# Gate steps of the expert stage on TensorE: run in pairs behind two U blocks each, instead of one behind each U block

## The reference, cut to what matters

```
def block(xb):
    qh = (xb @ w_pq).reshape(PEER_BLOCK, PEER_HEADS, 2, PEER_HALF)
    s = jnp.einsum('thcd,ckd->thck', qh, sub_keys).astype(jnp.float32)
    s_top, i_top = lax.top_k(s, PEER_TOPK)
    cand = (s_top[:, :, 0, :, None] + s_top[:, :, 1, None, :]).reshape(...)
    best, ci = lax.top_k(cand, PEER_TOPK)
    e = (i_top of half 0 at ci // 16) * N_KEYS + (i_top of half 1 at ci % 16)
    gw = jax.nn.softmax(best, axis=-1)
    act = jax.nn.gelu(jnp.einsum('tkd,td->tk', u_tab[e], xb)) * gw
    return jnp.einsum('tk,tkd->td', act, v_tab[e])
```

## Time and profile before

| | us |
|---|---|
| median of 2 runs | 2036.71 |
| the two runs | 2034.24 and 2039.18 |
| the profiled execution | 2032.12 |
| its span, first to last instruction | 2030.4 |

### The profile page before, as it was taken

One profiled execution on the slowest core, in us unless ns is written; L12 is line 12 of the kernel. 1 busy time (PEld: TensorE's weight loads), 2 busy tenths in 40 slices (PEclk: granted clock), 3 DMA queues, 4 the chain that ended last, 5 costly groups with the idle time before them and its releaser, 6 DMA issues.

```text
span 2030.4 us, 28703 instructions
## 1 busy us (share of the span) xinstructions
PE 1912.2 (94%) x10526; PEld 1606.1 (79%) x10526; DVE 1356.0 (67%) x2554; ACT 726.4 (36%) x967; POOL 706.6 (35%) x506
## 2 busy tenths in 40 slices
PE   5999977597999999999999999999999999999998
PEld 4999544386888888888888878878888888888886
DVE  4343658465198887779679787457666666666676
ACT  3113117441234453453455345423232232232232
POOL 2001200010146665776776677433222222222221
PEclk8999987798999999999999999999999999999999
DMA  8335833631236795996898699999888888888882
GB/s 324 94 99 34 306 122 138 222 111 52 70 132 205 271 362 194 348 378 229 295 372 328 221 347 369 325 358 355 300 288 282 299 287 281 300 287 281 297 289 95
DMA packets 220530, 504.91 MB, mean 249 GB/s; under 512 B 32200, under 2 KB 100040, under 8 KB 215184
## 3 DMA queue, kind: packets, MB, share of 16 engines
q1 hardware_dynamic: 176224, 319.03, 47.6%
q0 software_dynamic: 41472, 151.01, 20.2%
q10 hardware_dynamic: 2736, 33.60, 4.0%
HBM read 426.72 MB, written 76.57 MB: 248 GB/s over the span
## 4 chain that ended last, share of the span: by engine, by line
PE 58%; DVE 4%; DMA 4%; POOL 3%; ACT 2%; SPq 1%; issue 1%; ACTq 0%; POOLq 0%; DVEq 0%
PE experts_ps L1892 33%; PE experts_ps L1871 23%; DMA u_raw<-in_uT 4%; PE experts_ps L1883 2%; POOL u_low L183 2%; ACT u_high L1960 1%; SPq L1794 1%; PE experts_ps L1859 1%; ACT token_gates L2032 0%; DVE s_vr L2213 0%; DVE whot L2217 0%; POOL gather_rows L1735 0%; DVE oN L2161 0%; DVE wb L2199 0%; DMA s_vr<-in_v_tab 0%
## 5 line engine op out<-in xcount | busy, mean ns | idle before, releaser
L1871 PE MATMUL experts_ps<-h2h,u_high 128*128 128x480 f32 x1024 | 396.1, 387 | 6.8 <-POOL u_low L183 6.8
L1892 PE MATMUL experts_ps<-s_vh,s_ah 128*128 128x512 f32 x1024 | 399.4, 390 | 3.1 <-DVE s_al L2266 3.0
L1892 PE MATMUL experts_ps<-s_vh,s_al 128*128 128x512 f32 x1024 | 399.1, 390 | 0.0
L1892 PE MATMUL experts_ps<-s_vl,s_ah 128*128 128x512 f32 x1024 | 398.9, 390 | 0.0
L183 POOL TENSOR_TENSOR u_low<-u_raw,u_high 128x1024 fp32r<-128x1024 f32 x128 | 312.0, 2438 | 229.9 <-ACT u_high L1960 173.5
L1871 PE MATMUL experts_ps<-h2h,u_low 128*128 128x480 f32 x1024 | 388.3, 379 | 0.0
L1871 PE MATMUL experts_ps<-h2l,u_high 128*128 128x480 f32 x1024 | 388.1, 379 | 0.0
L1723 POOL DMA_INDIRECT gather_rows<-in_v_tab,expert_index x128 | 160.3, 1253 | 514.3 <-DVE u_raw L2275 493.9
L1984 ACT CAST s_vh<-s_vr 128x1024 fp32r<-128x1024 f32 x128 | 134.8, 1053 | 460.2 <-PE experts_ps L1892 457.7
L2264 DVE TENSOR_TENSOR s_vl<-s_vr,s_vh 128x1024 fp32r<-128x1024 f32 x128 | 156.7, 1224 | 204.7 <-ACT s_vh L1984 204.7
L1892 PEld LDWEIGHTS experts_ps<-s_vh,s_ah 128*128 128x128 f32 x1024 | 192.5, 188 | 43.9 <-DVE s_al L2266 3.4
(11 more groups left out here) (411 smaller groups left out, 2773.6 us busy)
## 6 DMA issues: line engine op xcount, KB each, us to landing
u_raw<-in_uT SPq DMA_DIRECT2D x128, 512.0 KB, 4.6
s_vr<-in_v_tab SPq DMA_DIRECT2D x128, 512.0 KB, 5.1
scratch_HG<-s_ar SPq DMA_DIRECT2D x128, 256.0 KB, 5.7
scratch_G<-token_gates ACTq DMA_DIRECT2D x16, 2048.0 KB, 10.4
s_ar<-scratch_HG SPq DMA_DIRECT2D x128, 256.0 KB, 4.2
token_gates<-scratch_G SPq DMA_DIRECT2D x30, 1024.0 KB, 10.4
mod_first<-in_w_ada SPq DMA_DIRECT2D x4, 2048.0 KB, 9.7
wa_second<-in_w_ada SPq DMA_DIRECT2D x4, 2048.0 KB, 8.1
```

Source lines behind the costliest of these rows:

```text
L1871: mm = pe.matmul(hP[:, slot, 0:NDENSE], w[:, slot, k, :], x[:, k, 0:NDENSE], start=(k == 0 and w is u.high and x is m.h2h), stop=(k == KD ...
L1892: mm = pe.matmul(yP[:, y, :], a[:, s, t * P:(t + 1) * P], v[:, s, d], start=(start and a is ah and v is vh), stop=(stop and v is vl))
```

## The change

TensorE's program is written in another order; no instruction is added or taken away, and no other engine's program changes. Gate step n of an even q is no longer issued behind its own U block. Both steps of a pair are issued behind the U block of the odd q. All four counts of steps in a tile are even, so every step has its pair, 32 pairs in all.

```diff
@@ -1939,7 +1939,9 @@
                             pe.wait_ge(t_taken, ND)
                             pe.transpose(tP[:, 0:P], x_act[:, :], m.ident[:, :]).then_inc(t_made, 1)
                         hidden(step_block(r, q))
-                        token_step(first_step(r) + q)
+                        if q % 2:
+                            token_step(first_step(r) + q - 1)
+                            token_step(first_step(r) + q)
                 for n in range(last_step + 1, NKEY):
                     hidden(n)
```

## The result

The changed kernel takes 2218.22 (median of 2 runs, 2217.11 to 2219.32) against 2036.71: 181.5 more, ratio 1.0895 (95% interval 1.0866 to 1.0923). The forecast was 2190 with a range up to 2214, so the time lies 4 above the range.

A forecast was written before the change was run, and what follows sets the result against it. TensorE was taken as the bound, with pairs making it wait for POOL's low parts. 125.5 without clock loss plus 28 for the clock gave 153.5, so 2185.6 on the profiled execution, named as 2190; range 2152 to 2214.

The forecast's parts named there:

- the clock's price: U blocks behind the 28 pauses: lower TensorE clock costs 0 to 1.58 each, taken as 1.0, 28 in all (0 to 44).
- The low part at T + 6.15: T is the start of a pair's first gate step; the next U block's low part is ready 6.15 later.
- behind the last pair of a tile: Top U block there waits for gate copies, starting at T + 3.2 instead of T + 1.84: 4 x 1.3 = 5.2.
- 125.5 for all but the clock: Whole kernel: sum of all terms without clock loss, 119.8 + 5.2 + 2.5 + 1 - 3.
- the slow steps of before: Steps where a late U load delayed ACT, with most waits for gate copies, would go: -3.
- 119.8: Late low parts between pairs within tiles: 4.28 more per pair, 28 times.
- at the heads and in the last steps: Tile heads: first gate step no longer fills a wait, 2.5; last steps: low parts 0.6 later, about 1.
- the pause of 2.63: Earlier pause in the trace before the change, after which the clock stayed at 1.00; evidence that a pause may cost nothing.
- its second rival: Full clock price at every pair's pause: 125.5 + 44 = 170 more, 2206; chance 0.18.
- The one without loss of clock: Two half gate steps keep the clock up in the pauses: 125.5 more, 2162; chance 0.18.
- The one with the full price: Clock falls late enough to lie in the U block on every pair: 2206; chance 0.18.
- That the second U block of a pair waits as well: Its 0.31 of room is gone, so it waits 1 to 2: 42 on top, about 2232; chance 0.05.

The follow-up runs named there:

- The filling experiments: Changed kernel with 12, 6, 3 or 1 extra matmuls ahead of the 28 U blocks behind a pause: 2164.4, 2162.3, 2178.3, 2220.6.
- e1_fill12: Changed kernel with 12 extra matmuls ahead of each of the 28 U blocks behind a pause, before the wait for the low part: 2164.4.
- e1b_fill6: Changed kernel with 6 extra matmuls ahead of each of the 28 U blocks behind a pause: 2162.3.
- e2_high_first: Changed kernel with the 16 high-part products first in each U block and the wait for the low part behind them: 2099.8, ratio 1.0304.

## Why the prediction was wrong

**The step that failed is the clock's price**, "So each costs between 0 and 1.58. I take 1.0 ... 0 and 44". It measured 2.07 in the mean and 58.0 in all, 30 above the value taken and 14 above the end of the bounds. I had one U block behind a long pause and took its loss for the most that such a block can lose. In that row the clock was at the lower level for 3.4, all of it inside the U block. In the changed kernel 14 of the 28 falls are like that one and cost 1.54 in the mean; the other 14 last for 6.8 and cost 2.61. The prediction also counted on the fall lying partly in the pause, where it costs nothing. It does, by 0.6 to 2.2 in the long ones, but 4.7 to 6.2 of them still lie in the U block. The upper end could have been had from the rows of before: a whole block at half the clock would cost about as much again as it takes, 5.2 (an estimate; in the row from 749.70 the matmuls take 0.40 each instead of 0.22).

The filling experiments show that this is the clock: with the same order, waits and pair loop, 12 more matmuls make the kernel 54 faster. What decides between 3.4 and 6.8 stays open. In all 28 places the long falls began 0.6 to 2.2 ahead of the U block, the short ones between 0.5 ahead of it and 0.7 behind its start.

**The rest of the sum held.** The low part at T + 6.15 and the U block at T + 6.20 came out at T + 6.11 and T + 6.16; a pair without loss of clock takes 16.7, as said (e1_fill12). The halves of the second gate step started at T + 1.89 and T + 2.70 against 1.9 and 2.8; behind the last pair of a tile the U block starts at T + 3.13, against 3.2. 125.5 for all but the clock and 58.0 for the clock make 183.5, and the stretch grew by 183.0. That the two agree to 0.5 is in part luck, since the small terms are off by more and cancel: the slow steps of before, put at -3, add up to 4.5 in the trace and are all gone, and 28 x 4.23 = 118.4 stand in the place of 119.8, against a little more at the heads and in the last steps.

**The rule on pauses.** The clock fell at all 28 pauses of the changed kernel, and the pause of 2.63 that I set against that did not carry over. By the section of the Trainium skill on HAM oscillation ("TensorE: Matmul & The Clock Gate") pauses between bursts bring the lower clock back each time. The trace agrees at these 28. The prediction had this as its second rival, with a chance of 0.18, and weighed it too low. The 28 shorter idle pieces of 1.5 in e1b_fill6 were followed by a slow U block only twice.

**The rivals.** The one without loss of clock (2162) is what e1_fill12 and e1b_fill6 measure, 2164 and 2162, but only with filling. The one with the full price had the right mechanism with too small a price (2206). That the second U block of a pair waits as well did not happen: even in e1_fill12, where no slow clock hides it, two U blocks ran through in 10.68.

In e2_high_first a forecast failed that had taken both the late U loads and the loss of clock as gone. The loads were only covered, and came back as soon as the cover was taken away, and with their waits came falls of the clock. That same cover is why the slow steps are gone in the changed kernel.

## What to carry to other kernels

When steps of two kinds alternate on the bound engine, each kind is the time in which the other engines prepare the other one: before two of a kind are put together, count from the end of the first how long the chain on the other engines takes to the next thing that is needed, since with two buffers it can't start earlier. Ask for an operand as late as its first use: that order of products gave 7 us here, a third of a per cent, for nothing. If a pause of a few us is repeated, don't take the one pause that the old trace happens to show for the most that it can cost. The upper end is the whole piece of work that follows at the lower level (here 5.2; 1.3 to 2.9 were measured). Useless matmuls in the pause show what the clock's share is. And look at the clock behind every wait of that length, whoever is waited for.

## What was unexpected of the hardware

A pause of 2.8 in which the engine was fully idle, with 2.2 of sparse gate steps ahead of it, made the clock fall to 0.50 in 28 of 28 places, for 3.4 in half of them and 6.8 in the others, mostly by turns, with 2.07 of loss for each U block in the mean. 1.3 of filling right ahead of the idle piece (6 matmuls, 1.5 idle left) kept it up in 26 of 28; 0.65 (3 matmuls, 2.1 left) kept it up in 19 of 28 in its fastest run, with 20 us between runs of one kernel; 0.2 (1 matmul, 2.6 left) did nothing.

A load of 512 KB issued 0.20 behind a store of 2 MB landed after 10.31, where the median of such loads is 4.5 (e2_high_first).
